# A fused transformer step on one NeuronCore: order of the first norm, pieces of the modulation, and a compact fold of the second modulation

## The reference, cut to what matters

```
mod = silu(cond) @ w_mod + b_mod            # six vectors of 1024 per condition (context, latent)
shift1, scale1, gate1, shift2, scale2, gate2 = mod
x  = LN_in(x [+ position embedding of the latent tokens])
u  = x * (1 + scale1) + shift1
out = TokenMix(u)          # projections q, k, v, o, gates; mLSTM in two directions; Fourier and pooling
                           # branches; merge by sigmoid gates; output projection w_out
x  = LN1(alpha * x + gate1 * out)           # weights g1, b1
u2 = x * (1 + scale2) + shift2
x  = LN2(alpha * x + gate2 * MoE(u2))       # 16 experts, top group, then two experts of it
```

## Time and profile before

| | us |
|---|---|
| median of three runs | 1081.48 (1080.07 to 1081.59) |
| profiled execution, own time | 1078.64 |
| its span in the trace | 1076.8 |
| PE busy | 999.3 (93% of the span) |
| DVE busy | 683.0 (63%) |
| ACT busy | 445.4 (41%) |
| POOL busy | 183.4 (17%) |

### The profile page before, as it was taken

How to read it: one execution, slowest core, us unless ns; L and a number is a source line. 1 busy time by engine, 2 the same in 40 slices (tenths; PEclk the granted TensorE clock), 3 DMA queues, 4 the chain that set the end, 5 groups by cost and what they waited for, 6 DMA issues and landing times.

```text
span 1076.8 us, 13573 instructions
## 1 busy us (share of the span) xinstructions
PE 999.3 (93%) x4659; PEld 773.5 (72%) x4659; DVE 683.0 (63%) x956; ACT 445.4 (41%) x626; POOL 183.4 (17%) x209
## 2 busy tenths in 40 slices
PE   6898999999999999699988998799999999999883
PEld 2698998577777777566656874588888888888741
DVE  5787671044263555825678568496799964799628
ACT  1632221144343424212050003476688853778523
POOL 2115511021000000101125531211111101010030
PEclk9899998999999999899999999999999999999987
DMA  9955450241211204614262035695999988699572
GB/s 335 353 213 193 173 197 14 78 147 23 76 48 71 79 1 184 226 59 138 68 220 93 20 140 192 209 387 185 383 399 398 399 310 292 231 399 398 205 264 120
DMA packets 84839, 213.21 MB, mean 198 GB/s; under 512 B 6912, under 2 KB 7190, under 8 KB 84800
## 3 DMA queue, kind: packets, MB, share of 16 engines
q1 hardware_dynamic: 66000, 149.45, 37.7%
q0 software_dynamic: 14512, 48.51, 13.0%
q10 hardware_dynamic: 4288, 14.72, 3.5%
HBM read 189.54 MB, written 23.11 MB: 197 GB/s over the span
## 4 chain that ended last, share of the span: by engine, by line
PE 76%; DVE 13%; ACT 4%; DMA 3%; issue 2%; POOL 1%; ACTq 0%; DVEq 0%; POOLq 0%
PE ps L1925 28%; PE ps L1686 21%; PE ps L1574 6%; PE ps L1672 5%; PE ps L1801 2%; PE ps L1917 1%; PE ps L1740 1%; ACT w_hi L831 1%; DMA R_d<-in_w_mod 1%; PE ps L1977 1%; PE ps L1795 1%; PE ps L1790 1%; DMA R_m<-in_ln_b 1%; PE ps L1952 1%; PE ps L1584 1%
## 5 line engine op out<-in xcount | busy, mean ns | idle before, releaser
L1686 PE MATMUL ps<-w_hi,uT_hi 128*128 128x512 f32 x320 | 132.1, 413 | 4.5 <-ACT R_x L896 2.6
L1686 PE MATMUL ps<-w_lo,uT_hi 128*128 128x512 f32 x320 | 126.4, 395 | 0.0
L1148 DVE TENSOR_TENSOR w_lo<-ring,w_hi 128x1024 fp32r<-128x1024 f32 x52 | 62.1, 1229 | 33.1 <-ACT w_hi L831 32.0
L1387 DVE TENSOR_TENSOR wa_lo<-ring,wa_hi 128x1024 fp32r<-128x1024 f32 x64 | 74.1, 1220 | 3.6 <-ACT wa_hi L948 3.1
L1686 PEld LDWEIGHTS ps<-w_hi,uT_hi 128*128 128x128 f32 x320 | 60.6, 190 | 21.7 <-issue 5.2
L1686 PEld LDWEIGHTS ps<-w_lo,uT_hi 128*128 128x128 f32 x320 | 60.5, 189 | 13.5
L1925 PE MATMUL ps<-wa_hi,xgT_hi 128*128 128x512 f32 x152 | 62.6, 412 | 5.2 <-DVE xgT_lo L1494 5.2
L896 ACT ACTIVATE R_x<-ps 128x512 f32<-128x512 f32 x30 | 17.9, 596 | 115.9 <-PE ps L1686 115.9
L1686 PE MATMUL ps<-w_hi,uT_lo_a 128*128 128x512 f32 x160 | 63.8, 399 | 0.0
L1686 PE MATMUL ps<-w_hi,uT_lo_b 128*128 128x512 f32 x160 | 62.3, 389 | 0.0
L948 ACT CAST wa_hi<-ring 128x1024 fp32r<-128x1024 f32 x64 | 62.2, 1048 | 0.0
(11 more groups left out here) (403 smaller groups left out, 2316.8 us busy)
## 6 DMA issues: line engine op xcount, KB each, us to landing
ring<-in_w_up SPq DMA_DIRECT2D x64, 512.0 KB, 8.6
ring<-in_w_in SPq DMA_DIRECT2D x11, 2048.0 KB, 10.4
R_d<-in_w_up SPq DMA_DIRECT2D x32, 512.0 KB, 10.8
R_p<-in_w_down SPq DMA_DIRECT2D x32, 512.0 KB, 9.5
R_h<-in_w_down SPq DMA_DIRECT2D x32, 512.0 KB, 10.1
y_slots<-R_m ACTq DMA_DIRECT2D x19, 512.0 KB, 6.3
ring<-in_w_mod SPq DMA_DIRECT2D x8, 1024.0 KB, 14.2
R_s<-in_w_up SPq DMA_DIRECT2D x16, 512.0 KB, 10.0
```

The lines of the kernel that those rows point to most:

```text
L1148: tt(lo[:, at], weights(name)[:, at], hi[:, at].bitcast(F32), ALU.subtract).then_inc(S["w_split"], 1)
L1387: tt(w_hi_lo[i][1][:, at], stage(i, q), w_hi_lo[i][0][:, at].bitcast(F32), ALU.subtract).then_inc(S["up_split"], 1)
L1686: i = mm(out, parts(k)[a][:, tok(j)], w[b][:, k], start=(k == 0 and a + b == 0), stop=(k == KD - 1 and b == 1))
```

## The change

- Start: position rows are loaded ahead of the first tile; idle products, then two position products, stand ahead of the first transpose; statistics of tiles 0 and 1 come ahead of the conditioning chain on DVE. The `gb` rows are made between the modulation halves, in banks 2 and p4, and their copies on ACT come behind that of chunk 0 and ahead of the square root, whose table is loaded early; DVE copies chunk 1 and makes both column groups ahead of `affine`. Eight idle products are added round the second fold.
- `affine` of tiles 2 to 4 moves behind the gate rows of the first half; the spill is split (tiles 0 and 1 behind the load of fp, 2 to 4 behind that of k), and DVE waits for the latter ahead of the scans.
- The padding is cleared ahead of POOL's pieces 3 and 4. The first row sum moves behind v.
- No pieces in the loop over the `o` tiles: pieces 16 to 31 all run in merge steps 20 to 28. Row sum 2 stays ahead of step 24, its eviction is in step 25; row sum 3 is behind step 29.
- scale2 and shift2 are folded with g1 and b1 on the compact row (128 x 512) in step 25, stored, and loaded as `mul2` and `add2`. The folds on 128 x 1024 go. The gate rows and the folded rows have semaphores of their own. POOL's affine of the first norm follows each tile's u2, that of the last tile the first gather.
- One pass for the router's logits, the first gather takes its indices without a copy, and the waits for the last affine move to the expert loop (ACT) and the final norm (DVE). The idle products (14, 16, 10 and 18 rows of the trace) stay.

Cut to its core:

```diff
@@ ACT and DVE, start
+            chain(nc.scalar.activation(scratch1[:, 0:1], const("one"), ACT.Sqrt), wait=False)
             evict_mod(0)
+            for i in range(4):
+                evict_rows(i)
             act.wait_ge(S["var_ready"], 1)
...
-            evict_mod(1)
             evict_mod(2)
...
+            take(dve, ("mod", 1))
+            release(nc.vector.tensor_copy(mod_part[1], bank(1)), ("mod", 1))
+            affine_columns(0)
             was_read(dve, ("gb", 3))
+            affine_columns(1)
             affine(0)
-            affine_columns(0)
             affine(1)
-            affine(2)
-            affine_columns(1)
-            affine(3)
...
             gate_rows(1, 0)
             gate_rows(0, 0)
-            affine(NT - 1)
+            for j in range(2, NT):
+                affine(j)
...
             stt(rows[2], rows[1], -1.0, rows[1], ALU.mult, ALU.max).then_inc(S["abs_ready"], 1)
+            dve.wait_ge(S["x_spilled4"], 48)
             dve.wait_ge(S["ln_ready"], 1)
@@ PE, start
-            for c_ in range(3):
-                modulation(c_)
-                if c_:
-                    fold_columns(c_ - 1)
+            modulation(0, 0)
+            modulation(0, 1)
+            pe.wait_ge(S["gb_row_loaded"], 32)
+            spread_row(0)
+            spread_row(1)
+            fold_columns(0)
+            modulation(1, 0)
+            spread_row(2)
+            spread_row(3)
+            modulation(1, 1)
+            was_read(pe, ("pos", 2))
+            idle_products(4, 5, P)
+            fold_columns(1)
+            modulation(2, 0)
+            idle_products(4, 5, P)
+            modulation(2, 1)
             pe.wait_ge(S["xn_ready"], NT)
@@ SP
-                    sp.wait_ge(S["x_ready"], NT)
-                    sp.dma_start(x_spill[tok(NT - 1), :], x_tok[:, NT - 1]).then_inc(S["x_spilled4"], 16)
+                    for j in range(2, NT):
+                        sp.wait_ge(S["x_ready"], j + 1)
+                        sp.dma_start(x_spill[tok(j), :], x_tok[:, j]).then_inc(S["x_spilled4"], 16)
@@ POOL
-            load_mod_pieces(3, 5)
             pool.wait_ge(S["x_ready"], NT)
             zp_clear = nc.gpsimd.memset(R_m[:, pad0:pad0 + 6 * PADW], 0.0)
             chain(zp_clear)
+            load_mod_pieces(3, 5)
...
             for j in range(NT):
-                pool.wait_ge(S["x1_pre"], j + 1)
-                chain(nc_t(x_tok[:, j], resid[:, j % 2], ROW1["g1"], ALU.mult))
-                nc_t(x_tok[:, j], x_tok[:, j], ROW1["b1"], ALU.add).then_inc(S["x1_ready"], 1)
                 pool.wait_ge(S["u2_ready"], j + 1)
                 pool.dma_start(u2_rows[tok(j), :], u2[:, j % 2]).then_inc(S[f"u2_stored{j % 2}"], 16)
+                if j < NT - 1:
+                    first_norm_affine(j)
...
-            gather(0)
+            gather_rows(tile_idx[:, 0:1])
+            first_norm_affine(NT - 1)
@@ DVE, merge steps
                 i.then_inc(S["ya_ready"], 1)
-                mod_pieces(16 + j, 17 + j)
-            late = {20: (21, 22), 21: (22, 23), 22: (23, 25), 23: (25, 26), 25: (26, 28), 26: (28, 30), 27: (30, 32)}
+            late = {20: (16, 18), 21: (18, 20), 22: (20, 22), 23: (22, 24), 25: (24, 25), 26: (25, 27), 27: (27, 29), 28: (29, 32)}
...
-                if s in (24, 28):
-                    mod_evict(2 if s == 24 else 3)
+                if s == 25:
+                    mod_evict(2)
+                    was_read(dve, ("rowsum", 2))
+                    dve.wait_ge(S["fold_rows"], 128)
+                    ch(stt(fold_add, mod_row[2], 1.0, fold_add, ALU.add, ALU.mult))
+                    ch(stt(fold_mul, mod_row[2], 1.0, fold_mul, ALU.add, ALU.mult))
+                    tt(fold_add, fold_add, mod_row[1], ALU.add).then_inc(S["fold_ready"], 1)
@@ DVE, out stage
-            dve.wait_ge(S["rows1_loaded"], 16 * 5)
-            ch(ts(ROW1["scale2_0"], ROW1["scale2_0"], 1.0, None, ALU.add))
-            ch(tt(u2[:, 0], ROW1["b1"], ROW1["scale2_0"], ALU.mult))
-            ch(tt(ROW1["shift2_0"], ROW1["shift2_0"], u2[:, 0], ALU.add))
-            ch(tt(ROW1["scale2_0"], ROW1["scale2_0"], ROW1["g1"], ALU.mult))
+            mod_evict(3)
@@ PE, merge steps
             for s in range(20, 30):
-                if s in (24, 29):
-                    sum_rows(2 if s == 24 else 3)
+                if s == 24:
+                    sum_rows(2)
                 merge_step(s)
+            sum_rows(3)
```

More of the change, by code:

```diff
@@ L119, in plan_psum @@
         fill(("modcol", c), "b3")
+        fill(("gb", c), ("b2", "p4")[c % 2])
     for d in range(KD):
@@ L163, in plan_psum @@
         fill(("yT", h, 0), ("b3", "p5", "p7")[h % 3])
-    for v in range(2, 4):
-        fill(("rowsum", v), "p4")
+    fill(("rowsum", 2), "p4")
     for s in range(20, 30):
@@ L168, in plan_psum @@
         fill(("Y", s), "b1")
+    fill(("rowsum", 3), "b0")
     for d in range(KD):
@@ L720, in _ @@
             for s in (1, 0):
                 take(pool, ("mT", KD - 1, s))
[L722 to L729, removed]
+            load_rows1(("gate1_1",), "gate_row1")
@@ L782, in _ @@
             nc.scalar.activation(silu_t, vecT[:, 0:16], ACT.Exp, scale=-1.0).then_inc(S["exp_cond"], 1)
-            for i in range(4):
-                take(act, ("gb", i))
-                release(nc.scalar.copy(gb_in[:, i], bank(2 + i % 2)), ("gb", i))
+            chain(nc.scalar.activation(scratch1[:, 0:1], const("one"), ACT.Sqrt), wait=False)
             def evict_mod(i):
@@ L789, in evict_mod, with evict_rows @@
                 release(nc.scalar.copy(mod_part[i % 2], bank(i % 2)), ("mod", i))
+            def evict_rows(i):
+                take(act, ("gb", i))
+                release(nc.scalar.copy(gb_in[:, i], bank(gbank(("gb", i)))), ("gb", i))
             evict_mod(0)
+            for i in range(4):
+                evict_rows(i)
             act.wait_ge(S["var_ready"], 1)
@@ L1061, in norm_stats, with in_stats @@
                 ch(nc.vector.bn_aggr(mv[:, 2 * jj:2 * jj + 2], stats))
-            dve.wait_ge(S["consts_loaded"], 16)
+            dve.wait_ge(S["consts_loaded"], 32)
+            def in_stats(j):
+                dve.wait_ge(tile_loaded[j], 32 if j == 1 else 16)
+                if j:
+                    take(dve, ("pos", j))
+                    release(tt(x_tok[:, j, 0:BW], x_tok[:, j, 0:BW], bank(3 + j), ALU.add), ("pos", j))
+                    ch(tt(x_tok[:, j, BW:D], x_tok[:, j, BW:D], pos_cols, ALU.add))
+                    was_read(dve, ("pos", j))
+                norm_stats(x_tok[:, j], j)
+            in_stats(0)
+            in_stats(1)
             take(dve, "vec")
@@ L1395, in _ @@
             dve.wait_ge(S["wr_loaded"], 16 * 4)
-            dve.wait_ge(S["x1_ready"], NT)
             remainder_up(0, 0, range(2))
             take(dve, "lg")
-            for j in range(NT):
-                i = tt(logits[:, j], bank(1)[:, j * 20:(j + 1) * 20], b_r, ALU.add)
-            release(i, "lg")
+            release(tt(logits, bank(1)[:, 0:NT * 20].rearrange("p (j n) -> p j n", j=NT),
+                       b_r.rearrange("p (j n) -> p j n", j=1).to_broadcast([P, NT, 20]), ALU.add), "lg")
             was_read(dve, "lg")
@@ L1477, in _ @@
             ts(plan[:, MAXT + 1:MAXT + 2], tile_end[0:1, NE - 1:NE], 1.0, None, ALU.subtract).then_inc(S["plan_ready"], 1)
+            take(dve, "slots")
+            release(nc.vector.tensor_copy(tile_idx[:], bank(1)[:, 0:MAXT]), "slots")
             dve.wait_ge(S["route_exp"], 1)
@@ L1575, in product, with idle_products, spread_positions @@
                 return i
-            pe.wait_ge(S["consts_loaded"], 16)
+            pe.wait_ge(S["consts_loaded"], 32)
+            def idle_products(n, b=7, width=BW):
+                for _ in range(n):
+                    mm(bank(b)[:, 0:width], ident, consts[:, 0:width], start=True, stop=True)
+            def spread_positions(j):
+                name = ("pos", j)
+                begin(pe, name)
+                filled(mm(bank(3 + j), pos_rows[:, BW + (j - 1) * P:BW + j * P], pos_rows[:, 0:BW], start=True, stop=True), name)
+            idle_products(6, 0, P)
+            spread_positions(1)
+            spread_positions(2)
             pe.wait_ge(S["vec_loaded"], 112)
@@ L1875, in route @@
                     filled(i, "lg")
-            def idle_products(n):
-                for _ in range(n):
-                    mm(bank(7), ident, consts[:, 0:BW], start=True, stop=True)
             for j in range(NT):
```

162 lines of the change are left out of this document (81 added, 81 removed).

## The result

The changed kernel is slower by 0.33%: a median of 1083.84 over 20 runs (1080.12 to 1087.87) against 1079.70 for the kernel before over 20 runs (1076.46 to 1085.02); the ratio is 1.0033, 95% interval 1.0017 to 1.0049. The prediction was 1078.8 and faster. What a single trace adds of its own is told where it shows.

A forecast was written before the change was run, and what follows sets the result against it. PE, busy 93% of the span, was taken as the bound, leaving its pauses, lower clock, start and end. Terms 8 - 9 + 7 - 8.8 - 5 + 9.5 + 1 = +2.7 gave 1075.9 profiled, 1078.8 median; range 1071 to 1086.

The forecast's parts named there:

- the start, +8: Start up to the gate products: filled PE pauses and earlier copies gain 8 us (+2 to +9.3).
- rival (b): Start stays at the lower clock, gate products near 45.6, gain only +2, whole 1084.8; chance 0.20.
- The bound: Start limited by weight arrival and the work behind it: gate products at 38.3 at best, a gain of 9.3.
- In front of k, -9: Wait before the first k product: DVE waits for three spill stores, k later, loss of 9 us (-5 to -14).
- Rival (a): Spill stores get a fair DMA share and land at 79, k term -5, whole 1074.8; chance 0.20.
- the 2.3 for POOL's chain: In front of k: POOL's pooled chain running while DVE splits k slows DVE by about 2.3 us.
- The padding's memset: Before k: the moved memset (3.48) no longer stands between pieces and copies, but ends no wait.
- Heads, +7: Behind the scans: with pieces out of the loop, the 9.8 wait falls to about 2.9, gain 7 (+6.5 to +7.6).
- Step 24, -8.8: Row sum ahead of step 24 waits 6.4 for later pieces, plus lower clock: loss of 8.8 (-6.4 to -9.3).
- Step 29, -5: Last merge stands behind three pieces and the out split: 3.4 plus 1.6 for the clock, loss of 5 (-3.4 to -7).
- Out projection, +9.5: Wide second-modulation folds go, with tile 0's wait of 4.4 and the low clock after it: gain 9.5 (+8.5 to +10.1).
- Routing, +1: Gather issued some 3.6 earlier, but kept idle products limit the gain to 1 (0.2 to +1.3).

The follow-up runs named there:

- 4b: Changed kernel with row sum behind step 24, pieces spread, zeros behind spill stores, affine 2 and 3 earlier, row products in one block: 0.9782 to the kernel before.
- 3b: Changed kernel with its four row products in one block ahead of the modulation, ACT's copies ahead of chunk 0's: 0.9979 to the kernel before.
- 2c: Kernel before with only the padding cleared ahead of POOL's loads of pieces 3 and 4: 0.9954 to the kernel before.
- 1c: Changed kernel with seven idle products in PE's pause ahead of the row sum of step 24: 1.0023 to the kernel before.
- 2a: Changed kernel with POOL issuing its 4.6 MB of zeros only after the three spill stores have landed: 1.0013 to the kernel before.
- 1a: Changed kernel with PE's row sum of the third vector behind step 24 instead of ahead of it: 0.9939 to the kernel before.

## Why the prediction was wrong, point by point

**The step that failed is the start, +8.** I took the full clock for granted there because most of PE's pauses would be filled. They were filled (PE runs from 18.23 to 46.24 without one), and yet the clock came to its full level only at 35. The place of the row products kept it there, though why is not shown: with the rows between the modulation halves the full level came at 35 to 43 in six executions, with the same rows in one block at 24.9 and 29.5 (4b and 3b), without them at 22.0 to 29.9. The gate products began at 46.2 to 50.3 (before: 47.60, and 45.03 in the second trace of that start), so the term was +1.4 in the profiled execution and about -2 over the executions seen (means of 48.7 and 46.3). This is rival (b) in its condition, the lower clock, and it had a chance of only 0.20. Its price (45.6 against 46.24, normalisation at 32.2 against 32.43) came near by luck: it went by ACT's copies holding PE up, and PE never waits for ACT there; its own products at the lower clock fill the time. With the block the term is 5.4 (3b, 42.22) and 7.5 (4b, 40.08) against the trace of before. The bound was too early too: its terms add up to 38.45, and it put 20 transposes at 1.3 where 16 take 1.97 at the full level (43.62 in the changed kernel's trace).

**In front of k, -9:** right in kind, -5 in size (4.2 of pause, 0.8 of clock). Rival (a) held here: stores at 80.5 (it had 79), share 47.1%. And the 2.3 for POOL's chain fell on POOL. The padding's memset, put at nothing because the store wait covers it, is worth 5 where no such wait stands (2c). The forecast of k itself was 18.6 behind the stores: 80.5 + 18.6 = 99.1 against 99.0 (97.65 + 1.36).

**Heads, +7:** 6.4, with 3.3 left where 2.9 was forecast. The low clock that reaches into step 20, -1.8, was not counted; it stands in this one trace of eleven with that loop.

**Step 24, -8.8:** 8.2 (6.5 and 1.7; 1c gives the clock 1.8). Undoing it gave 10. **Step 29, -5:** 4.5 of pause and 1.7 of clock, 1.4 of it given back by the row sum that no longer stands ahead of step 29.

**Out projection, +9.5:** 7.2 (13.92 to 6.75); the wait and the low clock after it went as forecast, but three short low stretches at 574 to 636 stand in the trace after, of which I had counted none (before, there is one such stretch at 625). **Routing, +1:** -0.6, as the kept idle products are now the last thing in the way.

A further 1.9 went at 226 us, where a wait of 1.3 for ACT (0.8 before) was followed by 3.4 at the lower level. No part of the change is at that place, and only this trace and one other (at 212.6) show such a stretch; its cause is left open.

With +1.4 for +8 and the other terms as forecast the sum is -3.9: slower. The other misses (k +4.0, heads -2.4, step 24 +0.6, step 29 +0.2, out -2.3, routing -1.6, the units -1.9) make -3.4 together, and -7.3 is what the traces differ by at the gathered rows (7.37). The medians differ by 4.1. The 1.8 behind the heads and the 1.9 at 226 us belong to this execution and account for most of that gap. Over the executions seen, with -2.3 for the start and without these two, the terms give -7.3 where the medians give -4.1; the start of before is known from two traces only, so the account by medians does not close to better than some 3. Either way the start's miss, 6.6 to 10, is by itself enough to turn +2.7 into a loss.

## What to carry to other kernels

Before a term counts on the clock's full level, look at what PE does in that stretch, product by product: the same row products cost some 6 us more between the modulation products than ahead of them. When work is moved out of a wait, find every in-order consumer in front of which it now ends (here a row sum one step too early), and place it so that the consumer comes one step later. A new wait for a store costs from the last write that it covers (5.6 in 2a), so the last producer is what must be early.

## What the runs showed of the hardware that was not expected

- The same four one-partition row products and eight halves of modulation products: with the rows in one block ahead of them the full clock level comes at 24.9 and 29.5 us, interleaved at 35 to 43. Windows of 1a (interleaved), where the trace has the records:

```profile
24.00:36.00 12.00, 12.00 (x42) 6.00 (x41) 2.34 (x7) 5.13 (x7) 0.00 (x0) 0.50 1.05 387
36.00:44.00 8.00, 8.00 (x50) 5.26 (x50) 5.33 (x7) 3.26 (x5) 0.00 (x0) 0.71 0.67 253
```

PE was busy all 12 us of the first window and the clock stayed at 0.50, that is 1.2 GHz.

- Between DVE and POOL the one that has the start keeps going. Where POOL's chain began first, two DVE passes took 6.80 (2c); where DVE was already in a row of passes, POOL's first operation took 13.07 and DVE lost nothing (two passes in 2.46). The Trainium skill states this, page "SBUF — State Buffer", section "SBUF: two separate sides", of the port pair that the two engines share: whoever starts first holds it for the whole instruction. The traces agree (6.80 one way, 13.07 the other), and add that a row of DVE passes without a gap holds POOL for all of its length.
- A start of the same instructions varies: gate products from 46.24 to 50.28 in six executions with the changed start. One trace of each kernel is not enough for a term of 4 us there.
